# Sending tokens to experts through scratch rows in device memory in a two-layer decoder step

## The reference, cut to what matters

```python
def moe_swiglu(h, w_router, b_router, w_gate_up, w_down):
    logits = (h @ w_router).astype(jnp.float32) + b_router.astype(jnp.float32)
    top_val, top_idx = lax.top_k(logits, TOP_K)              # TOP_K = 2
    top_w = jax.nn.softmax(top_val, axis=-1)
    gates = jnp.sum(jax.nn.one_hot(top_idx, N_EXPERTS, dtype=jnp.float32) * top_w[..., None], axis=-2)
    y = jnp.zeros_like(h)
    for e in range(N_EXPERTS):                               # 8 experts, w_gate_up[e] 1024 x 7168, w_down[e] 3584 x 1024
        y = y + gates[..., e:e + 1] * swiglu(h, w_gate_up[e], w_down[e])
    return y
...
        x = x + g2[:, None, :] * f                           # f = moe_swiglu(...), g2 comes from the conditioning vector
...
    shf, scf = jnp.split(jax.nn.silu(c) @ p['final_ada_w'] + p['final_ada_b'], 2, axis=-1)
    y = modulate(rmsnorm(x, p['final_norm']), shf, scf)      # rmsnorm(x) * (1 + scf) + shf
```

## Time and profile before

| | |
|---|---|
| median of 3 runs | 1837.83 us (1836.67 to 1837.96) |
| profiled execution | 1840.57 us, its span 1838.8 us |
| PE, DVE, ACT, POOL busy | 92%, 70%, 61%, 6% |
| bytes moved by DMA | 523.04 MB, mean 284 GB/s |
| first expert product to last | about 756 to 1803 us of the span |

### The profile page before, as it was taken

The page is one execution under the profiler, slowest core; times in us unless marked ns, Lnnn a source line. Parts: engine busy times, 40 slices in busy tenths (PEclk is TensorE's granted clock), DMA queues, the critical chain, the costliest instruction groups (busy, mean ns, idle before and its releaser), DMA issues.

```text
span 1838.8 us, 26111 instructions
## 1 busy us (share of the span) xinstructions
PE 1693.3 (92%) x9440; PEld 1357.6 (74%) x9440; DVE 1294.3 (70%) x1630; ACT 1114.7 (61%) x1359; POOL 112.3 (6%) x138
## 2 busy tenths in 40 slices
PE   5799779999869896799999999999999999999995
PEld 2694269999758574588787787787787787887873
DVE  2463365554557342699898998998997998998983
ACT  2553144443434542577787777777777777777773
POOL 2000100000013001000000000000000000000000
PEclk8899889999989987799999999999999999999998
DMA  9266957545567985499899898998998998998980
GB/s 348 93 214 237 391 178 252 180 162 198 181 254 287 341 289 201 150 335 364 302 355 366 294 359 327 328 359 330 332 357 331 327 360 315 338 364 298 354 306 24
DMA packets 234613, 523.04 MB, mean 284 GB/s; under 512 B 5340, under 2 KB 27970, under 8 KB 234547
## 3 DMA queue, kind: packets, MB, share of 16 engines
q1 hardware_dynamic: 229202, 504.42, 76.3%
q0 software_dynamic: 5040, 16.62, 2.5%
q10 hardware_dynamic: 304, 1.08, 0.2%
HBM read 514.11 MB, written 8.00 MB: 284 GB/s over the span
## 4 chain that ended last, share of the span: by engine, by line
PE 76%; DMA 7%; DVE 7%; issue 5%; ACT 4%; POOL 0%; SPq 0%; DVEq 0%; ACTq 0%; POOLq 0%
PE psum L678 21%; PE psum L680 20%; PE psum L679 20%; PE psum L649 2%; DMA ring<-in_ada_w 2%; DMA ring<-in_moe_w_gate_up 2%; PE psum L1081 2%; DMA ring<-in_cache_k 2%; PE psum L1096 1%; PE psum L668 1%; DVE w_lo L1531 1%; DVE x L1618 1%; PE psum L633 1%; PE psum L1105 1%; DVE ring L1813 1%
## 5 line engine op out<-in xcount | busy, mean ns | idle before, releaser
L1973 DVE TENSOR_TENSOR w_lo<-ring,w_hi 128x1024 fp32r<-128x1024 f32 x672 | 815.9, 1224 | 120.3 <-ACT w_hi L1483 109.4
L1483 ACT CAST w_hi<-ring 128x1024 fp32r<-128x1024 f32 x672 | 704.3, 1053 | 230.5 <-PE psum L680 230.4
L678 PE MATMUL psum<-w_hi,xe_hi 128*128 128x512 f32 x896 | 371.0, 414 | 4.3 <-DVE w_lo L1973 4.3
L680 PE MATMUL psum<-w_hi,xe_lo 128*128 128x512 f32 x896 | 354.4, 396 | 0.0
L679 PE MATMUL psum<-w_lo,xe_hi 128*128 128x512 f32 x896 | 354.0, 395 | 0.0
L678 PE MATMUL psum<-hh,w_hi 128*128 128x264 f32 x864 | 252.6, 292 | 24.1 <-DVE w_lo L1531 20.7
L1531 DVE TENSOR_TENSOR w_lo<-ring,w_hi 128x1024 fp32r<-128x1024 f32 (+1 forms) x132 | 160.2, 1222 | 137.7 <-ACT w_hi L1195 137.6
L679 PE MATMUL psum<-hl,w_hi 128*128 128x264 f32 x864 | 249.2, 288 | 0.0
L680 PE MATMUL psum<-hh,w_lo 128*128 128x264 f32 x864 | 249.2, 288 | 0.0
L1195 ACT CAST w_hi<-ring 128x1024 fp32r<-128x1024 f32 (+1 forms) x132 | 135.7, 1034 | 118.2 <-PE psum L680 87.4
L678 PEld LDWEIGHTS psum<-w_hi,xe_hi 128*128 128x128 f32 x896 | 169.2, 189 | 41.8 <-DVE w_lo L1973 4.7
(11 more groups left out here) (309 smaller groups left out, 1678.0 us busy)
## 6 DMA issues: line engine op xcount, KB each, us to landing
ring<-in_moe_w_gate_up SPq DMA_DIRECT2D x112, 2048.0 KB, 7.9
ring<-in_moe_w_down SPq DMA_DIRECT2D x56, 2048.0 KB, 7.6
ring<-in_ada_w SPq DMA_DIRECT2D x24, 2048.0 KB, 11.1
ring<-in_ffn_w_gate_up SPq DMA_DIRECT2D x22, 1024.0 KB, 7.8
ring<-in_gla_w_in SPq DMA_DIRECT2D x6, 2048.0 KB, 10.9
ring<-in_kv_ada_w SPq DMA_DIRECT2D x4, 2048.0 KB, 8.2
ring<-in_ffn_w_down SPq DMA_DIRECT2D x4, 2048.0 KB, 8.0
ring<-in_kv_w SPq DMA_DIRECT2D x4, 2048.0 KB, 12.6
```

Source lines behind the costliest of these rows:

```text
L678: eng.matmul(to, wh, ah, start=start, stop=False)
L680: return eng.matmul(to, wl, ah, start=False, stop=stop)
L1483: eng.copy(unit(w_hi, kind, n), quarter(ring[(BASE + j // 4) % RING], kind, j % 4)).then_inc(S["hi_ready"], 1)
L1973: eng.tensor_tensor(unit(w_lo, kind, n), quarter(ring[(BASE + j // 4) % RING], kind, j % 4), unit(w_hi, kind, n), ALU.subtract).then_inc(S ...
```

## The change

Four scratch tensors are made in device memory. `routed` holds, for each expert, 264 rows of 1024; POOL writes zeros to the first 128 rows of each (eight stores of 512 KB, 4.19 MB) in front of the constants of the attention, and waits until they have landed. In the router the logits are eight matmuls with `w_router` as the stationary operand, turned by three small transposes; the 24 transposes of `h` to token rows stand next to them, kept by six ACT copies as `h_tok`; `ada(116, 128)` moves behind the counts on PE, ACT and DVE. DVE works out two lists of row numbers for each token, `row_of` (in `routed`) and `row_back` (in the results), and POOL sends `h_tok` to `routed` by six indirect transfers.

In the sparse arm `x` of the prompt tokens is turned once to token rows `x_tok` (16 transposes), and three vectors (the MoE gate, the final gain and the final shift) are turned, stored and loaded back as rows on all partitions (`row_bc`). POOL loads each expert's rows `xe_rows` (512 KB) from `routed`, and stores two results of an expert, `y_e` and `y_g` (`y_e` times the gate row, a 128x1024 product of DVE at unit 40), 512 KB each. PE turns `xe_rows` at unit 66, and ACT and DVE split it at unit 70. `gather`, `keep_rows`, `put`, `scatter` and `add_chunk` are gone. ACT loads its silu table ahead of the loop.

At the end six indirect transfers bring each token's two rows back into ring slots, DVE weighs and adds them to `x_tok`, and the final norm goes along token rows: squares summed by ACT, root, and two DVE steps for each of the two prompt tiles, stored by ACT's queue. The 8 sample tokens go through sixteen small matmuls. The general arm keeps the old tail. Some semaphores are merged into one that DVE counts its own steps with.

```diff
-SCATTER_AT, ADD_AT, PUT_AT = 4, 8, 32
+TURN_ROWS_AT, SPLIT_ROWS_AT, GATE_ROWS_AT = 66, 70, 40
...
+        routed = nc.dram_tensor("routed", [NE * T, D], F32)[:]
+        expert_out = nc.dram_tensor("expert_out", [NE * CAP, D], F32)[:]
+        expert_gated = nc.dram_tensor("expert_gated", [NE * CAP, D], F32)[:]
+        last_rows = nc.dram_tensor("last_rows", [3, D], F32)[:]
...
             eng.wait_ge(S["hl_ready"], (IN_FFN + 1) * KC)
+            eng.memset(zero_rows[:], 0.0).then_inc(S["consts"], 1)
+            eng.wait_ge(S["consts"], 12 + STRIPS)
+            for e in range(NE):
+                eng.dma_start(routed[e * T:e * T + CAP, :], zero_rows[0:CAP, :]).then_inc(S["routed_zero"], 16)
+            eng.wait_ge(S["routed_zero"], 16 * NE)
             eng.tensor_copy(ident_r[:], ident[:]).then_inc(S["att_consts"], 1)
             eng.tensor_scalar(sixty_fourth[:], ones[:], 1.0 / 64, None, ALU.mult).then_inc(S["att_consts"], 1)
             eng.tensor_scalar(never[:], neg_after[:], -NEVER, None, ALU.mult).then_inc(S["att_consts"], 1)
...
+            eng.wait_ge(S["h_tok_kept"], 2 * TT)
+            eng.wait_ge(S["rows_placed"], 1)
+            for t in range(TT):
+                for c in range(2):
+                    eng.indirect_dma_start(routed, row_index(row_of, t, c), h_tok[0:TOK[t], t, :], None).then_inc(S["rows_sent"], 16)
...
+                eng.wait_ge(S["rows_sent"], 16 * 2 * TT)
+                expert_rows(0)
+                eng.wait_ge(S["last_sent"], 16)
+                for n in range(3):
+                    eng.dma_start(row_bc[:, n, :], last_rows[n].partition_broadcast(P)).then_inc(S["last_spread"], 16)
+                eng.wait_ge(S["xe_turned"], 2)
+                expert_rows(1)
                 for e in range(NE):
-                    if e >= 1:
-                        eng.wait_ge(S["gather_done"], 2 * e)
-                    for t in range(TT):
-                        n = TOK[t]
-                        last = eng.tensor_scalar(pick[0:n, t, :], iota[0:n, :], pos[0:n, t, e:e + 1],
-                                                 chosen[0:n, t, e:e + 1], ALU.is_equal, ALU.mult)
-                    last.then_inc(S["pick_ready"], 1)
-                    if e >= 1:
-                        eng.wait_ge(S["put_turned"], e)
-                    for t in range(TT):
-                        n = TOK[t]
-                        last = eng.tensor_scalar(put_tok[0:n, t, :], iota[0:n, :], pos[0:n, t, e:e + 1],
-                                                 gate_tok[0:n, t, e:e + 1], ALU.is_equal, ALU.mult)
-                    last.then_inc(S["put_ready"], 1)
-                eng.wait_ge(S["gather_done"], 2 * NE)
-                eng.memset(pick[:].bitcast(F32), 0.0).then_inc(S["pick_ready"], 1)
...
+                    if e + 2 <= NE:
+                        eng.wait_ge(S["xe_turned"], 2 * (e + 2))
+                        expert_rows(min(e + 2, NE - 1))
+                    eng.wait_ge(S["y_e_kept"], e + 2)
+                    eng.dma_start(expert_out[e * CAP:(e + 1) * CAP, :], y_e[:]).then_inc(S["y_e_sent"], 16)
+                    eng.wait_ge(S["y_g_kept"], e + 2)
+                    eng.dma_start(expert_gated[e * CAP:(e + 1) * CAP, :], y_g[:]).then_inc(S["y_e_sent"], 16)
+                    eng.wait_ge(S["y_e_sent"], 32 * (e + 1))
+                    if e < NE - 1:
+                        eng.nop().then_inc(S["y_kept_free"], 1)
+                eng.wait_ge(S["lo_ready"], NE * (4 * PER_E) + NU)
+                for t in range(TT):
+                    for c in range(2):
+                        eng.indirect_dma_start(back[t][0:TOK[t], c, :], None, expert_gated if t < 2 else expert_out,
+                                               row_index(row_back, t, c)).then_inc(S[f"y_back{t}"], 16)
...
+            for k in range(KC):
+                eng.wait_ge(S["h_ready"], LONG_NO[FFN1] * KC + k + 1)
+                last = eng.matmul(pb[4][0:NE, 0:T], w_router[:, k, :], h[:, k, :], start=k == 0, stop=k == KC - 1)
+            last.then_inc(S["logits_done"], 1)
...
+            eng.wait_ge(S["lg_kept"], 1)
             for t in range(TT):
-                if t == 0:
-                    h_is_ready(FFN1)
-                for k in range(KC):
-                    last = eng.matmul(pb[4][0:TOK[t], t * NE:(t + 1) * NE], h[:, k, t * P:t * P + TOK[t]], w_router[:, k, :],
-                                      start=k == 0, stop=k == KC - 1)
-            last.then_inc(S["logits_done"], 1)
-            ada(116, 128, ends=True)
+                last = eng.transpose(pb[5][0:TOK[t], t * NE:(t + 1) * NE], lg8[:, t * P:t * P + TOK[t]], ident[0:NE, 0:NE])
+            last.then_inc(S["lg_turned"], 1)
+            for i in range(2, 2 * TT):
+                turn_h(i)
...
             last.then_inc(S["count_done"], 1)
+            ada(116, 128, ends=True)
...
+                eng.wait_ge(S["ada_kept"], 32)
+                for i in range(4):
+                    t, a = i // 2, i % 2
+                    for j in range(4):
+                        last = eng.transpose(pb[i][:, j * P:(j + 1) * P], x[:, 4 * a + j, t * P:(t + 1) * P], ident[:])
+                    last.then_inc(S["once_turned"], 1)
...
-                gather(0)
-                turn_gathered(0)
+                eng.wait_ge(S["expert_rows"], 16)
+                eng.wait_ge(S["once_kept"], 5)
+                turn_rows(0)
...
-                        if SCATTER_AT <= j < SCATTER_AT + KC:
-                            scatter(j - SCATTER_AT, it)
-                        if j == PUT_AT:
-                            eng.wait_ge(S["put_ready"], it + 1)
-                            eng.wait_ge(S["added"], it * 8 + 9)
-                            for t in range(TT):
-                                n = TOK[t]
-                                last = eng.transpose(pb[5][:, t * P:t * P + n], put_tok[0:n, t, :], ident[0:n, 0:n])
-                            last.then_inc(S["put_turned"], 1)
                         if j == 56 - 1:
-                            eng.wait_ge(S["put_kept"], it + 1)
-                        if j == 75:
+                            eng.wait_ge(S["y_e_kept"], it + 1)
+                        if j == TURN_ROWS_AT:
                             eng.wait_ge(S["at_lo_ready"], it * 7 + 7)
-                            eng.wait_ge(S["pick_ready"], it + 2)
-                            gather(it + 1)
-                        if j == 77:
-                            turn_gathered(it * 2 + 2)
+                            eng.wait_ge(S["expert_rows"], it * 16 + 32)
+                            turn_rows(it * 2 + 2)
+
+                eng.wait_ge(S["last_gains"], 1)
+                eng.wait_ge(S["y_back2"], 32)
                 for k in range(KC):
-                    scatter(k, NE)
...
+                    for c in range(2):
+                        last = eng.matmul(pb[4][:, k * NB:(k + 1) * NB], back[2][0:NB, c, k * P:(k + 1) * P], gate_s[:, c, :],
...
-            ada(116, 120)
+            eng.wait_ge(S["logits_done"], 1)
+            eng.copy(lg8[:], pb[4][0:NE, 0:T]).then_inc(S["lg_kept"], 1)
+            eng.preload_act_table_set("natural_log_exp_and_others")
+            for i in range(2 * TT):
+                t, a = i // 2, i % 2
+                eng.wait_ge(S["h_tok_turned"], i + 1)
+                eng.copy(h_tok[0:TOK[t], t, a * 512:(a + 1) * 512], pb[6 + i % 2][0:TOK[t], :]).then_inc(S["h_tok_kept"], 1)
...
-                            eng.wait_ge(S["added"], it * 8 + 1)
+                            eng.wait_ge(S["y_kept_free"], it + 1)
                             eng.copy(y_e[:], psum[:, 5 * 512:7 * 512]).then_inc(S["y_e_kept"], 1)
-                        if j == PUT_AT + 4:
-                            eng.wait_ge(S["put_turned"], it + 1)
-                            eng.copy(put[:], pb[5][:, 0:T]).then_inc(S["put_kept"], 1)
...
+                        if j == SPLIT_ROWS_AT:
                             keep_gathered(it * 2 + 2)
+                eng.preload_act_table_set("sqrt_and_others")
                 eng.wait_ge(S["unit_used"], NE * (4 * PER_E) + NU)
+                eng.wait_ge(S["y_kept_free"], NE + 1)
...
+                def gate_rows(lo, hi):
+                    return eng.tensor_tensor(y_g[:, lo:hi], y_e[:, lo:hi], row_bc[:, 0, lo:hi], ALU.mult)
...
-                        if ADD_AT <= j < ADD_AT + KC:
-                            add_chunk(j - ADD_AT, it)
-                for k in range(KC):
-                    add_chunk(k, NE)
...
+                        if j == GATE_ROWS_AT:
+                            eng.wait_ge(S["last_spread"], 48)
+                            eng.wait_ge(S["y_e_kept"], it + 1)
+                            gate_rows(0, D).then_inc(S["y_g_kept"], 1)
...
+                for t in range(2):
+                    eng.wait_ge(S[f"y_back{t}"], 32)
+                    link(eng.scalar_tensor_tensor(x_tok[:, t, :], back[t][:, 0, :], w1[:, t:t + 1], x_tok[:, t, :], ALU.mult, ALU.add))
```

(50 more changed lines are left out.)

245 lines of the change are left out of this document (143 added, 102 removed).

## The result

The changed kernel takes 1775.10 us (median of four, 1773.87 to 1776.82) where the one before took 1837.89 beside it: the ratio is 0.9655, 95% interval 0.9643 to 0.9666. The forecast was 1756 with a range of 1742 to 1784. The sign and the range held; the kernel is 19 us slower than forecast, so that much of the gain did not come. The profiled execution took 1775.70 us, its span 1774.0.

The account below looks back on a forecast made before the run. PE was taken to set an expert's pace while DVE and loads keep up. Loop −74.5, router −12, tail −4 and zero rows +8 make −82.5 on 1840.57: 1758.1, told as median 1756 us, range 1742 to 1784.

Parts of the forecast that it names:

- The loop: Eight experts: period falls from 130.44 to 121.1 us as gather, scatter and put go, −74.5 us in all.
- 84 units × 1.395: Expert loop: PE's units in one expert, at the unit time of the earlier profile, take 117.2 us.
- DVE: Expert loop: DVE's work, 114.9 of 121.1 us, fits; the rival that it binds gave 1776 us, chance 0.06.
- The loads: Expert loop: 45.6 MB in 121.1 us need 377 GB/s, under the 390 seen, so cost 0; the term in doubt.
- The rival of 1794 us: Expert loop: loads are the ceiling at 362 GB/s, +38 us on the forecast; chance 0.14.
- the slower one: Expert loop: POOL's transfers starve the ring, 337 GB/s, 135.3 us an expert, 1870 us in all; chance 0.04.
- The router: From the router to the first expert product: ada piece moved behind the counts, start at 744.4, −12 us.
- The zero rows: Start of the dense SwiGLU: 4.19 MB of zero stores delay a ring load, +8 us, between 0 and 12.
- The tail: From the last y_e copy to the end: 36.2 us before, 32 after, −4 us.
- sample products and small steps 2.4: Tail: the sample tokens' products and small steps, behind the indirect gathers, take 2.4 us.
- the end of the program behind the last issue: Tail: what follows the final store, 4.2 us more, taken by difference from the profile before.
- The forecast's case: Whole kernel: all terms as summed, 1756 us; chance 0.50.

Follow-up runs that it names:

- the combined version: Changed kernel with clearing spread over the dense SwiGLU, sample rows fetched first in the tail, 96 bytes free ahead of xe_hi: 1738.58 us, 0.9457 of the kernel before.

## Why the prediction was right, and where it was off

**The loop** is off by 6.2 us, a term mis-sized. The mechanism (84 units, seven turns, eight transposes, and nothing else between PE's products) holds: PE is busy for 130.00 of 130.00 us in the window. What failed is the line "84 units × 1.395": it took the unit from the earlier trace rows as a property of the products, and the changed kernel runs them at 1.405. 84 × 0.010 × 8 = 6.7 us covers the miss. The two runs that gave the 1.395 back confirm it: with 8 words left free the eight experts take 971.4 us from the first product to the last copy of `y_e`, with the old address 972.3, and the forecast was 1046.1 − 74.5 = 971.6.

**DVE** was no bound: 114.9 of 121.1 was summed, and the unit buffers hid the gate row, as said.

**The loads** needed 377 GB/s and got them; of the two ends of the range was the one to take. The Trainium skill's limit of about 358 GB/s for one core ("DMA: Bandwidth & Descriptors", section Specifications) doesn't hold for this kernel: 372 to 376 in windows of 122 us over the six inner experts, 377 in the one shown, 385 to 390 with the added stores. The rival of 1794 us falls with it, and so does the slower one, which needed 347. (The loop alone would turn the sign at 350 GB/s, where a period is 130.44 us, and not at the 353 of the prediction; nothing hangs on it.)

**The router** came out at −11.3 for −12, and this closeness is in part luck, since several steps were off both ways. From ACT's first step of `h` on, in us:

| step | forecast | measured |
|---|---|---|
| logits complete | 5.1 | 6.2 |
| to `most` | 6.2 | 8.0 |
| ada piece | 11.3 | 11.0 |
| branch | 7.3 | 7.0 |
| transposes and last ACT copy | 6.4 | 4.3 |
| to the first expert product | 4.9 | 5.6 |

The eight logit matmuls were to end a microsecond behind ACT's scaling of `h`. They took 5.43 on the path, 0.68 each, more than the 0.5 of the ACT steps that feed them. Ahead of the counts a table load of 1.28 (ACT L1495) stands on the path, which the sum did not have: the transposes of `h` that PE does first wait for ACT's copies behind it. And ACT's part behind the branch ran on from 749.4 with the rows' copy, the store's issue and the table load of 1.28 that had been called gone from there: it had moved in front of the loop, onto the same path. Against this the sixteen transposes of `x` took 3.69, 0.23 each instead of 0.28. POOL's side was right in its price, one indirect transfer in 1.27 us on average (1.19 to 1.37 from one to the next, in both places) where 1.3 was taken between 0.52 and 3.38; the load of the first rows took 8.0 instead of 5.4 and came in level with PE's side, not hidden by 2.5 us.

**The zero rows** cost 9.8 us up to the router and 10.6 alone, for 8. Here the sum had let 1 MB slip into the window from 280 to 290. The window did rise from 286 to 382 GB/s, but the path hung on one tile of that traffic, and this tile got 9.15 us longer. The sentence on the Trainium skill's arbitration rule (same page, section Queues, rings and completion order) gave 10.7, and that was nearer. The runs agree with it in size; that the queues take turns by packet is not shown by them.

**The tail** failed in sign: +5.0 for −4. On the chain the step "sample products and small steps 2.4" took 8.1 us: sixteen products with eight columns in two passes each, 0.22 us a pass, on a PE that had idled since 1732.75 and whose granted clock was 0.50 (1.2 GHz) in these 7 us, and 1.1 us of small DVE steps. That is 5.7 of the 9. The remaining 3.3 are mostly in two terms. The store of `y_g` and the wait for it took 1 us more. And the end of the program behind the last issue, taken as 4.2 by difference, is mostly a closing drain, POOL's last long record in the trace, that lasts 6.12 us here and 4.07 before. The step of the sample products was sized by the work in it, from no row at all, while VectorE's queue held two finished tiles behind it: that is why another order gained 3 us.

**The chances.** The forecast's case happened in its mechanism, with the dearer clearing; none of the rivals did. Most of the miss came from two places to which no case was given: the placement of buffers (6.2 us) and small products on a PE at the lower clock (5.7). The drain at the end adds 2.0 and the clearing 1.8. The stages miss 17.7 us in all. Most of the rest of the 19 is the step from the profiled execution to the median, which was taken as 2.7 us and is 0.6 here.

## What to carry to other kernels

Work that only moves bytes should be placed by the transfer rate of the stretch it falls in, not by when its engine is free: here eight stores moved 30 to 110 us later gave back 10 to 12 us. When a change adds or moves buffers, compare the step of an unchanged inner loop before and after: if it has shifted by a per cent at the same clock, try other starts for the operands, since here 64 bytes were worth 12 us in one kernel, and the best start 19 us against the one it had by chance in the other (one run of that kernel; the combined version agrees with it). And size small steps in a tail by rows of the same engine at the clock that it is granted there, counting what is queued behind them.

## What the runs showed of the hardware that I had not expected

- A product of 128x512 in float32r steps in 228.8 to 234.1 ns at one granted clock, and most of it goes with where its stationary operands, and the buffers behind them, start within 128 bytes. In the kernel before the step of units 16 to 19 was 232.1 to 232.2 ns in five experts and 233.5 in three, with the same addresses, so the start isn't all of it.
- An indirect transfer of 128 rows of 4 KB costs POOL 0.94 to 1.07 us, one of 8 rows still 0.85 to 0.90, and the next one follows 0.30 later. In the tail the last landed 4.28 us behind its issue.
- POOL's closing drain, at the very end of the time that is measured, took 4.07 us in the kernel before, 4.72 with the clearing added, 5.96 with one stored result an expert, 6.12 in the changed kernel and 8.24 with four more stores an expert. It is longer the more transfers POOL has issued; by what rule is not shown.
- Products of eight rows and eight columns were not cheap on a PE that had been idle: 32 passes took 6.97 us at a granted clock of 0.50, about the time of five units of the expert loop, that is 30 products of 128x512 at full clock.
